# Two time directions in one product: the recurrence levels of a hybrid block on one NeuronCore

## The reference, cut to what matters

```python
def step(state, inp):                       # one chunk of tokens, G = cumsum(log f)
    qc, kc, ic, gc = inp
    G = jnp.cumsum(gc, axis=2)
    diff = G[:, :, :, None, :] - G[:, :, None, :, :]
    decay = jnp.exp(jnp.where(tri[:, :, None], diff, -jnp.inf))
    attn = jnp.einsum('bhtd,bhsd,bhtsd->bhts', qc, kc, decay)
    o = attn @ ic + jnp.einsum('bhtd,bhdv->bhtv', qc * jnp.exp(G), state)
    g_last = G[:, :, -1:, :]
    state = (jnp.exp(g_last[:, :, 0, :, None]) * state
             + jnp.einsum('bhsd,bhsv->bhdv', kc * jnp.exp(g_last - G), ic))
    return state, o
```

## Time and profile before

| what | before |
|---|---|
| median of 3 runs | 2360.72 us |
| the profiled execution's own time | 2358.43 us |
| its span, first to last instruction | 2356.6 us |
| mean granted TensorE clock | 0.994 |
| busy share PE / DVE / ACT / POOL | 97% / 68% / 34% / 48% |
| the recurrence with the gate products | about 512 to 816 us |

### The profile page before, as it was taken

The page is one execution under the profiler, slowest core; times in us unless marked ns, Lnnn a source line. Parts: engine busy times, 40 slices in busy tenths (PEclk is TensorE's granted clock), DMA queues, the critical chain, the costliest instruction groups (busy, mean ns, idle before and its releaser), DMA issues.

```text
span 2356.6 us, 29934 instructions
## 1 busy us (share of the span) xinstructions
PE 2295.6 (97%) x11150; PEld 1905.5 (81%) x11150; DVE 1600.4 (68%) x1953; ACT 791.8 (34%) x1056; POOL 1121.7 (48%) x886
## 2 busy tenths in 40 slices
PE   7999998999999999999999999899999999999998
PEld 5678887888888899887878888788888887779876
DVE  7899999965586354445586666877777602558787
ACT  4311241122333246412353333344433103344423
POOL 4235652333133246433478888898895432310130
PEclk9999999999999999999999999999999999999999
DMA  4021124432322412344234444744431311141231
GB/s 153 36 83 70 65 87 134 133 133 101 108 107 99 123 57 66 128 155 154 108 140 156 148 153 158 274 176 150 162 125 50 143 45 41 63 137 41 70 108 72
DMA packets 93266, 265.73 MB, mean 113 GB/s; under 512 B 8720, under 2 KB 26392, under 8 KB 87896
## 3 DMA queue, kind: packets, MB, share of 16 engines
q1 hardware_dynamic: 75216, 194.87, 23.9%
q10 hardware_dynamic: 17928, 69.23, 8.2%
HBM read 183.57 MB, written 81.80 MB: 113 GB/s over the span
## 4 chain that ended last, share of the span: by engine, by line
PE 77%; DVE 17%; issue 1%; DMA 1%; ACT 1%; POOL 0%; ACTq 0%; SPq 0%; DVEq 0%; POOLq 0%
PE pair L1066 31%; PE pair L1399 24%; DVE pen L2326 6%; DVE top L2324 6%; PE pair L1548 4%; PE pair L1307 2%; PE pair L1237 2%; PE pair L1517 2%; PE pair L1502 1%; PE pair L1084 1%; PE pair L1285 1%; PE pair L1274 1%; DVE tsp L2578 1%; PE pair L1276 1%; PE pair L1487 1%
## 5 line engine op out<-in xcount | busy, mean ns | idle before, releaser
L1066 PE MATMUL pair<-actA,w_hi 128*128 128x512 f32 x2016 | 626.0, 392 | 10.6 <-ACT stage L1665 7.8
L1066 PEld LDWEIGHTS pair<-actA,w_hi 128*128 128x128 f32 x2016 | 377.8, 189 | 90.2 <-ACT stage L1665 8.2
L915 POOL TENSOR_TENSOR pad<-pad 128x1 f32<-128x1 f32 x126 | 33.9, 269 | 799.5 <-PE pair L1066 704.5
L1066 PE MATMUL pair<-actA,w_lo 128*128 128x512 f32 x1008 | 393.4, 390 | 0.0
L1399 PE MATMUL pair<-tring,wsp 128*128 128x512 f32 x1344 | 307.4, 391 | 7.2 <-DVE tring L2651 5.7
L1399 PEld LDWEIGHTS pair<-tring,wsp 128*128 128x128 f32 x1344 | 253.1, 189 | 61.3 <-issue 8.0
L919 POOL TENSOR_TENSOR w_lo<-raw,w_hi 128x1024 fp32r<-128x1024 f32 (+2 forms) x126 | 275.7, 2188 | 10.1
L1066 PEld LDWEIGHTS pair<-actA,w_lo 128*128 128x128 f32 x1008 | 189.9, 188 | 39.9
L1399 PE MATMUL pair<-tsp,wsp 128*128 128x512 f32 x768 | 184.0, 391 | 3.9 <-DVE tsp L2578 1.9
L2619 DVE TENSOR_TENSOR xB<-pair,xB 128x1024 f32<-128x1024 f32 x112 | 136.4, 1220 | 71.0 <-PE pair L1399 70.6
L1066 PE MATMUL pair<-actB,w_hi 128*128 128x512 f32 x576 | 178.1, 390 | 0.0
(11 more groups left out here) (394 smaller groups left out, 4383.1 us busy)
## 6 DMA issues: line engine op xcount, KB each, us to landing
raw<-w_in SPq DMA_DIRECT2D x80, 512.0 KB, 3.2
wraw<-w_pair SPq DMA_DIRECT2D x32, 1024.0 KB, 7.1
staged<-hid_d SPq DMA_DIRECT2D x56, 512.0 KB, 3.2
proj<-stage ACTq DMA_DIRECT2D x40, 512.0 KB, 2.7
hid_d<-hsum SPq DMA_DIRECT2D x16, 1024.0 KB, 5.0
gates<-proj ACTq DMA_DIRECT2D x24, 512.0 KB, 5.5
raw<-w_out SPq DMA_DIRECT2D x16, 512.0 KB, 3.3
hid_d<-hid SPq DMA_DIRECT2D x16, 512.0 KB, 2.8
```

The source lines that it names most:

```text
L1066: last = nc.tensor.matmul(pair[par][:, cols], w[:, par, wk], x[:, cols], start=(k == 0 and i == 0), stop=(k == kt - 1 and i == 2))
```

## The change

Tokens 512 to 1023 are held backwards: ACT writes the second half of every q, f and i unit of the recurrence reversed into `stage` (two activations of 512 columns instead of one of 1024), and the log decay is cumulated from the far end. In a reversed chunk the early tokens stand at the high positions. So at each level the positions that are keys in a chunk of the first half are queries in a chunk of the second. The key factors of both halves then fill one operand of 512 columns, the query factors another, and one 128x128 product of chunk c holds the entries of chunk c above the diagonal and those of chunk 7 - c below it. A level is four products instead of eight; the diagonal stays at eight.

The exponents and weights write these dense operands and read the two halves in turn, m elements at a time, through hand-built views. `keep` collects the levels in `hC` (128 x 4 x 128): a copy for level 0, predicated copies after it, and at level 7 the upper triangle goes to chunks 0 to 3 of `hattn`, the lower to slots 4 to 7, and the diagonal to all. Slots 4 to 7 hold the chunks 7 to 4 (`slot_of`). The output products of these read their moving operand backwards, so that the output is in order again. The masks and the scan change to match.

```diff
-            for c in range(NB):
+            for c in range(NB // 2 if lv < LEVELS else NB):
                 cc = slice(c * P, (c + 1) * P)
                 mm = nc.tensor.matmul(mpair(key)[:, cc], ks[:, cc], qs[:, cc], start=True, stop=True)
...
-                        ks, qs = hW[:, lv % 2, :], hW[:, lv % 2, :]
+                        ks, qs = hW[:, lv % 2, 0:HALF], hW[:, lv % 2, HALF:S]
...
-                        mm = nc.tensor.matmul(out, hiT[:, c, :], hattn[:, c, :], start=True, stop=(c == 0))
+                        p = slot_of(c)
+                        way = slice(None, None, 1 if c < NB // 2 else -1)
+                        mm = nc.tensor.matmul(out, hiT[:, p, :], hattn[:, p, way], start=True, stop=(c == 0))
                         if c:
-                            mm = nc.tensor.matmul(out, hS[:, c, :], hqG[:, c * P:(c + 1) * P],
+                            mm = nc.tensor.matmul(out, hS[:, p, :], hqG[:, p * P:(p + 1) * P][:, way],
                                                   start=False, stop=True)
...
+                if turned:
+                    nc.scalar.activation(dst[:, 0:HALF], pair[par][:, 0:HALF], func)
+                    nc.scalar.activation(backwards(dst[:, HALF:S]), pair[par][:, HALF:S], func) \
+                      .then_inc(unit_out[par], 1)
...
-                        read_unit(a, par, hn, stage[:, s, :], funcs[s])
+                        read_unit(a, par, hn, stage[:, s, :], funcs[s], s < 3)
...
-                    V.tensor_tensor(dv[:, :, 1, :], gv[:, :, 1, :], mid, ALU.subtract)
-                    V.tensor_tensor(dv[:, :, 0, :], mid, gv[:, :, 0, :], ALU.subtract).then_inc(expo, 1)
+                    part = lambda x: dst[:, x * HALF:(x + 1) * HALF].rearrange("p (n x m) -> p n x m", x=2, m=m)
+                    G = hG[:, :]
+                    V.tensor_tensor(part(1), second_halves(G, m), middles(G, m, True), ALU.subtract)
+                    V.tensor_tensor(part(0), middles(G, m, False), first_halves(G, m), ALU.subtract) \
+                     .then_inc(expo, 1)
...
-                V.copy_predicated(hattn[:, :, :], hmask[:, lv:lv + 1, :].broadcast_to([P, NB, P]),
-                                  mpair(key)[:, :].rearrange("p (a b) -> p a b", b=P)).then_inc(F(key), 1)
+                found = mpair(key)[:, :].rearrange("p (a b) -> p a b", b=P)
+                mask = lambda j: hmask[:, j:j + 1, :].broadcast_to([P, NB // 2, P])
+                if lv == LEVELS:
+                    V.copy_predicated(hattn[:, 0:NB // 2, :], mask(LEVELS - 1), hC[:, :, :])
+                    step(V.copy_predicated(hattn[:, NB // 2:NB, :], mask(LEVELS), hC[:, :, :]))
+                    eye = C("ident").bitcast(I32).rearrange("p (o b) -> p o b", o=1)
+                    V.copy_predicated(hattn[:, :, :], eye.broadcast_to([P, NB, P]), found).then_inc(F(key), 1)
+                elif lv:
+                    V.copy_predicated(hC[:, :, :], mask(lv - 1), found[:, 0:NB // 2, :]).then_inc(F(key), 1)
+                else:
+                    V.tensor_copy(hC[:, :, :], found[:, 0:NB // 2, :]).then_inc(F(key), 1)
...
-                step(V.tensor_tensor_scan(hG[:, :], C("reset"), hE[:, 0, :], 0.0, ALU.mult, ALU.add))
+                reset = C("reset")[:, 0:HALF]
+                V.tensor_tensor_scan(hG[:, 0:HALF], reset, hE[:, 0, 0:HALF], 0.0, ALU.mult, ALU.add)
+                step(V.tensor_tensor_scan(backwards(hG[:, HALF:S]), reset, backwards(hE[:, 0, HALF:S]), 0.0,
+                                          ALU.mult, ALU.add))
...
-                    V.tensor_tensor(wv[:, :, 1, :], v(hq[:, 0, :])[:, :, 1, :], ev[:, :, 1, :], ALU.mult)
+                    V.tensor_tensor(part(hW, 1), second_halves(hq[:, 0, :], m), part(hE, 1), ALU.mult)
...
+def view(a, start, *dims):
+    return bass.AP(a.tensor, a.offset + start, [list(a.ap[0])] + [list(d) for d in dims])
...
+def first_halves(a, m):
+    return view(a, 0, (2 * m, HALF // (2 * m)), (HALF + m, 2), (1, m))
...
+def second_halves(a, m):
+    return view(a, HALF, (2 * m, HALF // (2 * m)), (m - HALF, 2), (1, m))
...
+def middles(a, m, second):
+    if second:
+        return view(a, HALF + m, (2 * m, HALF // (2 * m)), (-HALF - 1, 2), (0, m))
+    return view(a, m - 1, (2 * m, HALF // (2 * m)), (HALF + 1, 2), (0, m))
```

More of the change, by code:

```diff
@@ L122, in shape_constants @@
     masks = np.zeros((P, LEVELS + 1, P), np.int32)
-    for lv in range(LEVELS):
+    for lv in range(1, LEVELS):
         m = 64 >> lv
         same = (i[:, None] // (2 * m)) == (i[None, :] // (2 * m))
-        masks[:, lv, :] = same & ((i[:, None] // m) % 2 == 0) & ((i[None, :] // m) % 2 == 1)
-    masks[:, LEVELS, :] = np.eye(P, dtype=np.int32)
+        masks[:, lv - 1, :] = same & ((i[:, None] // m) % 2 != (i[None, :] // m) % 2)
+    masks[:, LEVELS - 1, :] = i[:, None] < i[None, :]
+    masks[:, LEVELS, :] = i[:, None] > i[None, :]
     return c, masks.reshape(P, -1)
@@ L350, in build @@
         hqG = at("hqG", 144, [P, S])
+        hC = at("hC", 174, [P, NB // 2, P])
         hy = at("hy", 203.5, [P, S])
@@ L675, in branch_out, with backwards @@
             return pair[1][:, (g % 2) * HALF:(g % 2) * HALF + 2 * P]
+        def backwards(x):
+            return x[:, ::-1]
         def by_key(x):
@@ L1246, in _ @@
                     for c in range(NB - 1):
-                        mm = nc.tensor.matmul(mpair(key)[:, c * P:(c + 1) * P], hkT[:, c, :], hiT[:, c, :],
+                        p = slot_of(c)
+                        mm = nc.tensor.matmul(mpair(key)[:, c * P:(c + 1) * P], hkT[:, p, :], hiT[:, p, :],
                                               start=True, stop=True)
@@ L1661, in _, with read_unit @@
                 hi_x(j)
-            def read_unit(n, par, hn, dst, func):
+            def read_unit(n, par, hn, dst, func, turned=False):
                 act.wait_ge(unit_mm, n + 1)
-                nc.scalar.activation(dst, pair[par][:, :], func).then_inc(unit_out[par], 1)
+                if turned:
[3 more added lines that the diff above has]
+                else:
+                    nc.scalar.activation(dst, pair[par][:, :], func).then_inc(unit_out[par], 1)
             for n in range(N_QK):
@@ L2337, in exponents @@
                     m = 64 >> lv
-                    gv = hG[:, :].rearrange("p (n x m) -> p n x m", x=2, m=m)
-                    dv = dst.rearrange("p (n x m) -> p n x m", x=2, m=m)
-                    mid = gv[:, :, 0, m - 1:m].broadcast_to([P, S // (2 * m), m])
-                    V.tensor_tensor(dv[:, :, 1, :], gv[:, :, 1, :], mid, ALU.subtract)
-                    V.tensor_tensor(dv[:, :, 0, :], mid, gv[:, :, 0, :], ALU.subtract).then_inc(expo, 1)
-                else:
-                    gv = hG[:, :].rearrange("p (n m) -> p n m", m=P)
-                    V.tensor_tensor(dst.rearrange("p (n m) -> p n m", m=P),
-                                    gv[:, :, P - 1:P].broadcast_to([P, NB, P]), gv,
+                    part = lambda x: dst[:, x * HALF:(x + 1) * HALF].rearrange("p (n x m) -> p n x m", x=2, m=m)
[3 more added lines that the diff above has]
+                     .then_inc(expo, 1)
+                else:
+                    blocks = lambda a: a.rearrange("p (e q n) -> p e q n", e=2, n=P)
+                    V.tensor_tensor(blocks(dst), last_steps(hG[:, :], P), blocks(hG[:, :]),
                                     ALU.subtract).then_inc(expo, 1)
@@ L2402, in _ @@
                     m = 64 >> lv
-                    v = lambda a: a.rearrange("p (n x m) -> p n x m", x=2, m=m)
-                    wv, ev = v(hW[:, lv % 2, :]), v(hE[:, lv % 2, :])
-                    V.tensor_tensor(wv[:, :, 1, :], v(hq[:, 0, :])[:, :, 1, :], ev[:, :, 1, :], ALU.mult)
-                    V.tensor_tensor(wv[:, :, 0, :], v(hk[:, :])[:, :, 0, :], ev[:, :, 0, :],
-                                    ALU.mult).then_inc(weighted, 1)
+                    part = lambda a, x: a[:, lv % 2, x * HALF:(x + 1) * HALF].rearrange("p (n x m) -> p n x m", x=2, m=m)
+                    V.tensor_tensor(part(hW, 1), second_halves(hq[:, 0, :], m), part(hE, 1), ALU.mult)
+                    V.tensor_tensor(part(hW, 0), first_halves(hk[:, :], m), part(hE, 0), ALU.mult) \
+                     .then_inc(weighted, 1)
                     if lv + 2 <= LEVELS:
@@ L2418, in _ @@
                 dve.wait_ge(decay, h * (LEVELS + 2) + LEVELS + 1)
-                step(V.tensor_copy(tiny[:, 0:8], hqG[:, P - 1:S:P]))
+                step(V.tensor_copy(tiny[:, 0:8].rearrange("p (e q n) -> p e q n", e=2, n=1), last_steps(hqG[:, :], 1)))
                 V.tensor_tensor(hqG[:, :], hqG[:, :], hq[:, 0, :], ALU.mult).then_inc(hfin, 1)
@@ L2433, in _ @@
                 for c in range(1, NB - 1):
-                    ins = V.scalar_tensor_tensor(hS[:, c + 1, :], hS[:, c, :], tiny[:, c:c + 1],
+                    p = slot_of(c)
+                    ins = V.scalar_tensor_tensor(hS[:, slot_of(c + 1), :], hS[:, p, :], tiny[:, p:p + 1],
```

(6 more changed lines are left out.)

## The result

The changed kernel takes 2334.65 us (median of four runs, 2334.2 to 2335.15) against 2360.44 us for the kernel before (2358.01 to 2361.09): the medians differ by 25.8 us. The estimated ratio of the two is 0.9899 with a 95% interval of 0.9887 to 0.9910, which is 23.8 us, with an interval of about 21 to 27. The prediction said 2335.9 us and 2333.5 to 2343.5. The profiled execution has a span of 2332.8 us, 23.8 less than before.

A forecast was written before the change was run, and what follows sets the result against it. TensorE's own time was taken as the bound of the recurrence stage. Span 2356.6 - 25.0 (removed passes) + 0.15 (ACT) = 2331.75 us, plus 1.8 and 2.3 gives 2335.9 us; range 2333.5 to 2343.5.

The forecast's parts named there:

- The bound and the main term: Recurrence stage: TensorE's own time is the bound; 224 passes removed at 0.1116 us each, 25.0 us less.
- The sum, term by term: Whole run: span 2356.6 - 25.0 + 0.15 = 2331.75 us, plus 1.8 and 2.3 gives 2335.9 us.
- All three hold: Covers before output products, level 1 and level 3, about 1 us each, suffice; 0 taken, up to 1 us a head at worst.
- the cover ahead of the output products: Head 2's turn: DVE's last state step ends 0.89 us before PE arrives at the output products; this cover stays.
- no idle PE ahead of levels 1: Sign the forecast is right: TensorE shows no idle time ahead of levels 1 and 3 or the output products.
- ACT: Evictions of q, f, i split in two; one is on the chain, +0.15 us, about +0.6 if backward writes run half rate.
- rival A: Output products: TensorE reads backwards at half rate, 64 passes double, +7.1 us, 2343.0 us; chance 0.07.
- The seam of the scan: POOL's w_lo gets in between the scan halves, swapping order with DVE; 0.2 to 0.4 of 0.89 us cover used.
- rivals B and C: DVE's hopping patterns cost double (B, 2338 to 2346, chance 0.10) or three times or more (C, 2368 at three, chance 0.03).
- rival B: DVE's interleaving patterns cost double, late at output products and level 3, 10 us back, 2346 us; chance 0.10.
- rival D: Start of attention: toep's landing set by traffic, not its issue; up to 25 us lost, 2360 us; chance 0.02.

The follow-up runs named there:

- e1: Kernel before with chunks 4 to 7 of levels 0 to 6 left out (products and their part of the predicated copies): 2334.28 us.
- e2: Changed kernel with each level product made twice, so TensorE has 8 products a level again: 2358.8 us, ratio to the kernel before 1.0004.
- e12: The changed kernel run once more, unedited, on the same chip: 2334.95 us, ratio to the kernel before 0.9902.
- e4: Kernel before with only the scan changed, made as two forward scans of 512 columns: 2358.31 us, ratio 1.0000.
- e10: Changed kernel with head 0's iT transposes one gate product earlier and ACT's split_qk behind the next units' first eviction: 2323.62 us.
- e5: Changed kernel with three more 512-column DVE operations ahead of the state recurrence of heads 0 to 2: 2339.34 us.

## Why the prediction was right

**The bound and the main term.** Right. 224 passes at 0.1116 us are 25.0 us; e1 (only these gone) and e2 (only these back) bracket it with stages of 391.3 and 414.8 us.

**The sum, term by term, in the stage.** 414.7 - 25.0 = 389.7 was due. Found: 391.5, and 391.1 in the second profile of the same kernel. The 1.4 us up to the latter are the two waits that I didn't see: head 0's level 1 on `hiT` (levels 0 and 1 together end 1.13 us later than two groups of 0.89 would, where the kernel before lost 0.24: 0.9) and the statistic's 3 x 0.16 = 0.5. Together 1.4. The last 0.4 us are in the gate products ahead of the levels (110.88 us against 110.53 before and 110.54 in e12), which the change doesn't touch: after its long wait TensorE was granted 0.50 of its clock for 2 us in all three, and then for 2 us 0.55 in the changed kernel's profile but 0.75 in the other two. Why it came back later there is open. So the step "All three hold" was right for its three places, though the cover ahead of the output products was 0.5 us and not 0.89, and the list of places was short by two: of the signs named, "no idle PE ahead of levels 1" failed in head 0. The sum was 1.4 us too good, and that the median came out 1.3 us below the forecast all the same is luck: the two medians differ by more than the stages do (25.8 against 23.2), within what the runs scatter.

**ACT.** The pair of halves took 0.60 + 0.50 = 1.10 us in the chain against 1.03: 0.07, where I took 0.15. The half written backwards (median 592 ns) is as fast as the forward one (597 ns).

**TensorE backwards (rival A).** Didn't occur. The output groups go from 579.46 to 582.80, 3.34 us, as before (3.35), with half their products read backwards.

**The seam of the scan.** As predicted: one w_lo, one change of places. The forecast was that 0.2 to 0.4 us of the cover would be used; e4 shows none used (states from 657.33 us, 657.39 before).

**The hop (rivals B and C).** Level 6 alone is slower, by 0.16 us per operation. The Trainium skill's rule (SBUF — State Buffer, "SBUF: two separate sides": at least two accesses to a 16-byte line, or a penalty) names the right level. It gives no size; here it was a quarter, not rival B's double. Even at all levels it costs 1.5 us, by way of the statistic and not at the places of rival B.

**Attention's door (rival D).** Didn't occur: from the end of head 3's statistic to the end of the span it is 1540.7 us before and 1539.8 after, and 1540.8 in e10, where the stage ends another 12 us sooner.

## What to carry to other kernels

Where one engine is busy throughout, count its passes and price them by their pitch in the chain; the rest is to check the covers. List the covers for both kinds of wait: results that come late, and buffers that are freed late. A group that is halved shortens the cover of whatever stands two groups behind it in the same PSUM tile. And look at the longest single wait of the bounding engine anywhere in the run: here one reordered line of ACT's queue was worth 9.4 us in the traces, two fifths of what the rewrite gave (23.2).

## What the hardware showed that I hadn't expected

- Reading the moving operand backwards costs TensorE nothing (3.34 against 3.35 us for the 30 passes of an output group); nor does a backward write on ACT (592 against 597 ns), or a backward scan on DVE (1.20 against 1.23 us, head 0).
- A float32 DVE operation of 512 columns whose reads hop by some 2 KB after every element took 0.81 to 0.85 us instead of 0.69, and one that hops after two was not slower (0.69, level 5).
- A wait before a TensorE group is felt from the first weight load on, which began 0.22 us ahead of the first matmul record and 0.38 us ahead of the group's share of the chain (649.47, 649.69, 649.85). The time lost is more than the wait that is listed: 1.33 us of wait and 0.26 us of longer passes in e5.
- After 7.8 us without work TensorE was granted 0.61 of its clock on average over 3.8 us (0.50 at first, then 1.00), which added 1.6 us to the gap's price.
